# A small two-layer network inside a long kernel: its first layer in single-pass matmuls, with the operands split into high and low parts beforehand

## The reference, cut to what matters

```
def compress_tokens(t, pos_emb, w1, w2):
    ...
    blocks = jnp.concatenate([chunks[:, :, i:i + n_cmp] for i in range(r)], axis=3)
    blocks = (blocks + pos_emb).reshape(B, G, n_cmp, CMP_BLOCK * dh)
    return jax.nn.gelu(blocks @ w1) @ w2
```

## Time and profile before

| | us |
|---|---|
| median of the runs | 964.74 |
| the profiled execution, its own time | 964.92 |
| its span | 962.7 |
| PE busy in the span | 946.2 (98%) |
| DVE, ACT, POOL busy | 569.4, 419.7, 369.0 |

### The profile page before, as it was taken

How to read it: one execution, slowest core, us unless ns; L and a number is a source line. 1 busy time by engine, 2 the same in 40 slices (tenths; PEclk the granted TensorE clock), 3 DMA queues, 4 the chain that set the end, 5 groups by cost and what they waited for, 6 DMA issues and landing times.

```text
span 962.7 us, 14693 instructions
## 1 busy us (share of the span) xinstructions
PE 946.2 (98%) x5579; PEld 823.8 (86%) x5579; DVE 569.4 (59%) x1083; ACT 419.7 (44%) x730; POOL 369.0 (38%) x442
## 2 busy tenths in 40 slices
PE   9999999999999999999999999999999999999997
PEld 8878887878888898688888888888999999988886
DVE  2764445388554356384558743888899999711114
ACT  5334325265555263345464633544444444433332
POOL 5771551246435454122223036597000000366561
PEclk9999999999999999999999999999999999999999
DMA  7374243112144252231211112226322442122312
GB/s 234 120 199 99 66 143 99 45 44 66 44 147 160 70 175 66 76 122 45 72 62 65 45 44 89 74 69 213 116 89 89 128 136 88 46 88 91 124 47 88
DMA packets 74758, 93.44 MB, mean 97 GB/s; under 512 B 15332, under 2 KB 53777, under 8 KB 74688
## 3 DMA queue, kind: packets, MB, share of 16 engines
q1 hardware_dynamic: 74256, 91.91, 29.9%
q10 hardware_dynamic: 432, 0.59, 0.2%
HBM read 90.09 MB, written 7.12 MB: 101 GB/s over the span
## 4 chain that ended last, share of the span: by engine, by line
PE 90%; DVE 4%; ACT 2%; issue 2%; DMA 1%; POOL 0%; SPq 0%; DVEq 0%; POOLq 0%; ACTq 0%
PE psum L1360 52%; PE psum L1421 17%; PE psum L1701 6%; PE psum L1661 4%; PE psum L1676 3%; PE psum L1753 1%; PE psum L1487 1%; PE psum L1627 1%; PE psum L1729 1%; PE psum L1743 1%; PE psum L1714 1%; DMA RAW<-in_w_in_dram 1%; PE psum L1640 1%; PE psum L1799 0%; DVE R L2730 0%
## 5 line engine op out<-in xcount | busy, mean ns | idle before, releaser
L1360 PE MATMUL psum<-WR,XT 128*128 128x512 f32 (+3 forms) x1620 | 390.5, 387 | 1.0 <-ACT R L1031 0.7
L2756 POOL TENSOR_TENSOR WR<-RAW,WR 128x256 fp32r<-128x256 f32 (+3 forms) x320 | 259.9, 841 | 321.0 <-ACT WR L1859 320.9
L1360 PEld LDWEIGHTS psum<-WR,XT 128*128 128x128 f32 x1620 | 285.9, 188 | 51.5 <-issue 4.1
L2756 POOL TENSOR_TENSOR WR<-RAW_B,WR 128x256 fp32r<-128x256 f32 x88 | 71.6, 837 | 202.7 <-ACT WR L1859 202.7
L1859 ACT ACTIVATE WR<-RAW 128x512 fp32r<-128x512 f32 (+3 forms) x160 | 93.4, 603 | 83.5 <-PE psum L1360 69.4
L1360 PE MATMUL psum<-WR,TT 128*128 128x512 f32 x528 | 119.9, 389 | 0.0
L1360 PEld LDWEIGHTS psum<-WR,TT 128*128 128x128 f32 x528 | 99.0, 188 | 20.5
L2034 ACT ACTIVATE prob<-prob,st 128x512 f32<-128x512 f32 (+2 forms) x112 | 58.4, 545 | 92.6 <-DVE st L2418 83.5
L1701 PEld LDWEIGHTS psum<-ones_up,probT 128*128 128x128 f32 x536 | 70.7, 191 | 7.1 <-issue 1.3
L1701 PE MATMUL psum<-ones_up,probT 128*128 128x128 f32 x536 | 72.7, 275 | 0.1
L1421 PE MATMUL psum<-TT,WR 128*128 128x256 f32 x576 | 71.7, 283 | 0.0
(11 more groups left out here) (292 smaller groups left out, 1254.0 us busy)
## 6 DMA issues: line engine op xcount, KB each, us to landing
RAW<-in_w_gate_up_dram SPq DMA_DIRECT2D x28, 512.0 KB, 5.0
RAW<-in_w_in_dram SPq DMA_DIRECT2D x13, 1024.0 KB, 5.2
RAW_B<-in_w_down_dram SPq DMA_DIRECT2D x11, 1024.0 KB, 5.0
RAW<-in_w_out_dram SPq DMA_DIRECT2D x8, 1024.0 KB, 5.3
RAW_B<-in_w_gate_up_dram SPq DMA_DIRECT2D x16, 512.0 KB, 6.0
RAW<-in_w_in_dram SPq DMA_DIRECT2D x13, 512.0 KB, 4.9
rep_scratch<-rows_scratch SPq DMA_DIRECT2D x12, 320.0 KB, 6.6
RAW<-in_w_in_dram SPq DMA_DIRECT2D x4, 768.0 KB, 4.3
```

The lines of the kernel that those rows point to most:

```text
L1360: last = pe.matmul(outp, stationary(x), moving(y), start=start and n == 0, stop=stop and n == 2)
L2756: last = pool.tensor_tensor(WR[:, s % RING, 1, lo:hi], raw[:, raw_half[g], q, lo:hi], WR[:, s % RING, 0, lo:hi].bitcast(F32), ALU.subtract)
```

## The change

- `hidden` is made of fp32r matmuls: the stationary operand is now 128 x 128, with the 64 columns of the blocks' high part beside the 64 of their low part, and the moving operand is once the high and once the low part of the `w1` piece. 16 pieces by 2 matmuls for each of k and v. The result has 128 rows: the lower 64 come from the blocks' high part and the upper 64 from their low part, and they have to be added.
- New steps `bp v`: ScalarE copies the high part of the blocks of k or v (128 x 1024), VectorE subtracts for the low part.
- New steps `w1 pair`, 16 of them: ScalarE copies two pieces' high part (128 x 512), VectorE subtracts for the low part, in place over `w1`. Pairs 0 to 7 are k, 8 to 15 v. `PLAN` puts 0 to 7 at quarters 16, 19, ... 37 of `in2` and 8 to 15 at 62 to 69.
- After part 1 of `hidden`: ScalarE copies rows 64 to 127 out, VectorE adds rows 0 to 63, ScalarE then takes the gelu (before: the gelu straight from PSUM).
- `qt cmp` and `blocks` stand two quarters earlier, `hidden` at (64, 66, 69, 72) where it was (64, 65, 67, 69), `hid_t` at (69, 75) where it was (67, 72). `w1` of k and v change places in SBUF, and so in the order of their DMAs.

```diff
     if kind == "hidden":
         kv, part = at
-        return [("hidden", kv, 0)] if part else [("hidden", 0, 1)] if kv else [("blocks",)]
+        out = [("w1", 4 * (2 * kv + part) + 3)]
+        return out + ([("hidden", kv, 0)] if part else [("hidden", 0, 1)] if kv else [("blocks",), ("bp", 1)])
+    if kind == "w1":
+        pair = at[0]
+        return ([("w1", pair - 1)] if pair else []) + ([("hidden", 0, 0)] if pair >= 12 else [("bp", pair // 2 - 4)] if pair >= 8 else [])
...
-                index["out1", 1, 0]: [load_x_again, lambda: load_w1(1)],
-                index["in2", 1, 0]: [lambda: load_w1(0)],
+                index["out1", 1, 0]: [load_x_again, lambda: load_w1(0)],
+                index["in2", 1, 0]: [lambda: load_w1(1)],
...
                     if part == 0:
                         wait_sc(step)
-                        pe.wait_ge(s_w1[kv], 16)
-                        pe.wait_ge(blk_done, 1)
+                        pe.wait_ge(blk_done, kv + 1)
+                    pe.wait_ge(w1_lo_done, 4 * (2 * kv + part) + 4)
                     for m in range(8 * part, 8 * part + 8):
-                        last = pe.matmul(SC[nth["hidden", kv, 0] % 2][0:64, 0:256], blocks[:, kv, m, :], w1[kv][:, m, :],
-                                         start=m == 0, stop=m == 15)
-                    if part:
-                        last.then_inc(sc_in, 1)
+                        for x, moving in enumerate((hi_of_w1(16 * kv + m), w1_lo[kv][:, m, :])):
+                            last = pe.matmul(SC[nth["hidden", kv, 0] % 2][:, 0:256], block_parts[kv][:, m, :, :].rearrange("p x n -> p (x n)"), moving,
+                                             start=(m, x) == (0, 0), stop=(m, x) == (15, 1))
+                    last.then_inc(sc_in if part else w1_used, 1)
...
+                elif what == "w1":
+                    pair = step[1]
+                    kv, m = divmod(2 * pair, 16)
+                    act.wait_ge(s_w1[kv], 16)
...
+                    if pair in (8, 10):
+                        act.wait_ge(blk_done, pair // 2 - 3)
+                    if pair == 12:
+                        act.wait_ge(w1_used, 1)
+                    act.activation(hi_of_pair(pair), w1[kv][:, m:m + 2, :], ACT.Copy).then_inc(w1_hi_done, 1)
+                elif what == "bp":
+                    v = step[1]
+                    act.wait_ge(blk_raw, v + 1)
...
+                    act.activation(block_parts[v][:, :, 0, :], blocks[:, v, :, :], ACT.Copy).then_inc(blk_hi, 1)
                 elif what == "hidden" and step[2]:
                     kv = step[1]
                     act.wait_ge(sc_in, nth["hidden", kv, 0] + 1)
-                    if kv == 0:
-                        act.wait_ge(tr_in, nth["qt", "cmp", 3] + 1)
-                    act.activation(hid_nat[0:64, kv, :], SC[nth["hidden", kv, 0] % 2][0:64, 0:256], ACT.Gelu_apprx_tanh).then_inc(hid_act, 1)
+                    act.activation(hid_nat[0:64, kv, :], SC[nth["hidden", kv, 0] % 2][64:128, 0:256], ACT.Copy).then_inc(hid_low, 1)
+
+                    act.wait_ge(sc_out, nth["hidden", kv, 0] + 1)
+                    act.activation(hid_nat[0:64, kv, :], hid_nat[0:64, kv, :], ACT.Gelu_apprx_tanh).then_inc(hid_act, 1)
```

More of the change, by code:

```diff
@@ L301, in make_timeline @@
         "OS": 1.5, "CS_b": 1.5, "F": 2, "sp_b": 2.5, "S": 3, "Z": 3, "sp": 4, "qt": 4.5,
-        "gx": 4.2, "xt": 4.4, "blocks": 5, "hidden": 6, "hid_t": 6.5, "gelu": 6, "cmpkv": 7, "gm_w": 8, "gm_a": 9, "gm": 10,
+        "gx": 4.2, "xt": 4.4, "blocks": 5, "bp": 5.2, "w1": 5.5, "hidden": 6, "hid_t": 6.5, "gelu": 6, "cmpkv": 7, "gm_w": 8, "gm_a": 9, "gm": 10,
     }
@@ L461, in make_timeline @@
         on(PLAN["hidden"][n], ("hidden", n // 2, n % 2))
+    for n in range(2):
+        on(PLAN["bp"][n], ("bp", n))
+    for pair in range(16):
+        on(PLAN["w1"][pair], ("w1", pair))
     for n in range(2):
@@ L997, in ones_and_v, with hi_of_w1, hi_of_pair @@
             return ones_up[:, 0:2 * at_].rearrange("p (x n) -> p x n", x=2)[:, :, 0:HD]
+        def hi_of_w1(n):
+            part, slot = ((1, 0), (0, 0), (0, 4), (2, 0), (3, 0), (3, 4), (0, 0), (0, 4))[n // 4]
+            return w1_hi[part][:, slot + n % 4, :]
+        def hi_of_pair(pair):
+            part, slot = ((1, 0), (0, 0), (0, 4), (2, 0), (3, 0), (3, 4), (0, 0), (0, 4))[pair // 2]
+            return w1_hi[part][:, slot + 2 * pair % 4:slot + 2 * pair % 4 + 2, :]
         def bias_of(name, h, i, m):
@@ L1258, in load_w1 @@
             def load_w1(kv):
-                if kv:
+                if not kv:
                     sp.wait_ge(tr_in, nth["F", 3, 2] + 1)
@@ L2055, in _ @@
                     take_transposed(act, step)
+                elif what == "w1":
+                    pair = step[1]
+                    kv, m = divmod(2 * pair, 16)
+                    act.wait_ge(s_w1[kv], 16)
+                    if pair == 0:
+                        act.wait_ge(sq_done, nth["sq", "in2", 3] + 1)
+                        act.wait_ge(gx_done, nth["gx", "in2", 3, 1] + 1)
+                    if pair in (8, 10):
[6 more added lines that the diff above has]
+                    act.wait_ge(blk_raw, v + 1)
+                    if v == 0:
+                        act.wait_ge(tr_in, nth["qt", "cmp", 3] + 1)
+                    act.activation(block_parts[v][:, :, 0, :], blocks[:, v, :, :], ACT.Copy).then_inc(blk_hi, 1)
                 elif what == "hidden" and step[2]:
@@ L2510, in _ @@
                                 last = dve.tensor_tensor(dst, s_, pp, ALU.add)
-                    last.then_inc(blk_done, 1)
+                        last.then_inc(blk_raw, 1)
+                elif what == "bp":
+                    v = step[1]
+                    dve.wait_ge(blk_hi, v + 1)
+                    dve.tensor_tensor(block_parts[v][:, :, 1, :], blocks[:, v, :, :], block_parts[v][:, :, 0, :].bitcast(F32),
+                                      ALU.subtract).then_inc(blk_done, 1)
+                elif what == "w1":
+                    pair = step[1]
+                    kv, m = divmod(2 * pair, 16)
+                    dve.wait_ge(w1_hi_done, pair + 1)
+                    dve.tensor_tensor(w1_lo[kv][:, m:m + 2, :], w1[kv][:, m:m + 2, :], hi_of_pair(pair).bitcast(F32),
+                                      ALU.subtract).then_inc(w1_lo_done, 1)
                 elif what == "hidden" and step[2]:
-                    dve.wait_ge(hid_act, step[1] + 1)
-                    dve.sem_inc(sc_out, 1)
+                    kv = step[1]
+                    dve.wait_ge(hid_low, kv + 1)
+                    dve.tensor_tensor(hid_nat[0:64, kv, :], SC[nth["hidden", kv, 0] % 2][0:64, 0:256], hid_nat[0:64, kv, :],
+                                      ALU.add).then_inc(sc_out, 1)
                 elif what == "hid_t":
```

22 lines of the change are left out of this document (17 added, 5 removed).

## The result

The changed kernel takes 974.94 us (median of four runs, 974.08 to 975.25), the kernel before 964.86 (four runs, 964.64 to 964.97): a ratio of 1.0103 [1.0086, 1.0121], 10.1 us slower. The direction was as forecast, the size was not: 4.1 us were forecast, and 974.9 lies outside 965.5 to 972.0.

What follows compares the result with a forecast made beforehand. TensorE was taken to bound the kernel, busy 946.2 of 962.7 us. Waits of 10.8 us less 6.7 us gained in `hidden` make +4.1, so 968.8 us, range 965.5 to 972.0.

Steps and rivals of the forecast that it cites:

- 1 chunk 0 to 1: At chunk 0's evacuation, split copies and subtractions queued ahead delay the first tiles on ScalarE and VectorE: 1.4 us.
- 2 `qt q 0`: At the first `qS` transpose, TensorE waits for chunk 1's tile 0, queued behind ScalarE's late `w1` copies: 0.6 us.
- 3 `qt q 1`: At the second `qS` transpose, TensorE waits for VectorE's subtractions, two tiles and `qS` copy: 0.7 us.
- 4 `qt q 3`: At the fourth `qS` transpose, TensorE waits for row copy, table load, sum, gelu and `qS` copies: 3.0 us, the largest.
- 5 `hid_t 0`: Behind the fourth `qS` transpose, its `qS` copies outlast the `hidden` matmuls running beside them: 0.8 us.
- 6 `qt slc 1`: At the second `kS_slc` transpose, no quarter covers copy, sum, gelu and the first transpose's copies: 2.0 us.
- 7 `hid_t 1`: Right behind `qt slc 2`, TensorE waits 1.0 us for copies, where it waited 0.5 before: cost 0.5 us.
- 8 `CS 0`: Ahead of `CS 0`, nothing covers VectorE placing the second layer's results: 2.3 us less 0.5 before, 1.8 us.
- first rival: VectorE and GpSimd block each other at chunk 0's evacuation; tile 1 starts 1.9 us later, 970.7 us; 0.19 shared with slower matmuls.
- rival with 384-column time: `hidden` matmuls paced like 384-column ones, gain 3.2 us instead of 6.7, up to 972.3 us; 0.19 shared with GpSimd lock.
- Hand-overs hidden: TensorE's work between transposes covers most of the ScalarE and VectorE waits, 7.6 us coming to nothing: 961.2 us; chance 0.13.
- Given back later: TensorE idle time elsewhere that hangs on its own clock, such as DMAs, absorbs the shift: no change, 964.8 us; chance 0.06.

Runs made afterwards that it cites:

- `fill`: Changed kernel plus 28 matmuls whose result nobody reads, ahead of the three long TensorE waits; 970.31 us, ratio 1.0058 to the kernel before.
- `plan2`: Changed kernel with another placing of the same steps and SP's bias loads behind chunk 3's first weight load; 967.55 us, ten runs.
- `order`: Kernel before, fp32 matmuls and no splits, with only the new places of `qt cmp`, `blocks`, `hidden` and `hid_t`; 972.56 us, ratio 1.0076.
- `plan3`: Changed kernel with steps placed so no idle times stand close together, `CS` from 83, bias loads behind the weight load; 963.80 us, ratio 0.9991.
- `keep`: Changed kernel, splits and single-pass matmuls kept, with `hidden` and `hid_t` back at their old places; 971.21 us, ratio 1.0068.
- `nov`: Changed kernel without the value weights' eight split pairs; `hidden` of the values uses the keys' parts, so values are wrong; 970.24 us, ratio 1.0064.
- `plan1`: Changed kernel with the same steps placed to give each transpose a quarter or more of cover, `CS` from 84; 974.62 us, ratio 1.0095.
- `plan1b`: `plan1` with SP's eight bias loads moved behind chunk 3's first weight load; 968.25 us, ratio 1.0042.
- `plan2f`: `plan2` plus 15 matmuls whose result nobody reads, ahead of four waiting TensorE instructions; 964.88 us, ratio 1.0000.

## Why the prediction came out as it did

| step | forecast | changed kernel | `fill` (clock at 1.00) |
|---|---|---|---|
| 1 chunk 0 to 1 | 1.4 | 1.4 | 1.4 |
| 2 `qt q 0` | 0.6 | 0.74 | 0.72 |
| 3 `qt q 1` | 0.7 | 0.68 | 0.68 |
| 4 `qt q 3` | 3.0 | 3.22 | 3.39 |
| 5 `hid_t 0` | 0.8 | 0 | 0.88 |
| 6 `qt slc 1` | 2.0 | 2.09 | 2.34 |
| 7 `hid_t 1` | 0.5 | 0.53 | 0.53 |
| 8 `CS 0` | 1.8 | 1.86 | 2.05 |
| sum of the waits | 10.8 | 10.5 | 12.0 |
| gain of `hidden` | -6.7 | -5.4 | -6.7 |
| what is left, half clock above all | 0 | 5.2 | 0 |
| shift of the far block | 4.1 | 10.3 | 5.3 |

For the changed kernel the gain is 1.3 less, since one part took 3.24 us, and 5.2 is what is left of the 10.3. For `fill` the wait of steps 4, 6 and 8 is the filling and the wait left behind it together (2.92 + 0.47, 2.10 + 0.24, and 2.09 + 0.47 less the 0.51 of before); the same wait unfilled reads about 0.2 less, because the profile counts idle time from the modelled end of a matmul. Its sum is 12.0 - 6.7 = 5.3, and `CS 0` was 5.32 late. The walk itself can so be followed to the tenth at full clock, and there it was 1.2 us short, over steps 2, 4, 5, 6 and 8.

*The step that failed* is the one that sums: waits of 10.8, "less 6.7 it makes +4.1 us". It priced an idle stretch of TensorE at its length and all matmuls behind it at the pace of the earlier trace rows. Nothing in the forecast, neither a term, nor a rival, nor the range, spoke of TensorE's clock, though the rows of before give it in a column of its own (1.00). The three stretches of step 4, 6 and 8 each brought the fall with them. That is 4.6 us of the 6.1 by which the forecast was short, as `fill` shows by the times; `plan2` with its two groups of runs bears the cause out. Most of the other 1.5 is the 1.2 by which the walked waits were short.

*Step 1* came out as forecast, at 1.4 us. TensorE in the changed kernel:

```profile
359.52 0.93 PE L1390 MATMUL psum<-WR,XT 128*128 128x512 f32 x3 [0.94 <-ACT st L1061]
361.04 4.49 PE L1390 MATMUL psum<-WR,XT 128*128 128x512 f32 x18 [0.59 <-DVE st L1061]
```

It waits 0.94 us for tile 0 and 0.59 for tile 1. Tile 0's quarter starts at 359.52, 0.63 after its 358.89; tile 1's at 361.04, in the kernel before at 359.65, three matmuls behind 358.89: 1.39 us late. The walk had 1.0 and then 0.4 more, so the sum is right in part by luck. VectorE in the changed kernel:

```profile
356.43 3.09 DVE L2574 TENSOR_TENSOR w_k_lo<-w_k,w_hi_a 128x512 fp32r<-128x512 f32 x3 [0.35 <-ACT w_hi_a L2098]
359.44 0.47 DVE L1061 TENSOR_SCALAR cmp_nat<-psum,st 128x256 f32<-128x256 f32 x1
```

The first three subtractions took 0.69 each, but the last three 3.09 us together (0.80, 1.23 and 1.22), so VectorE came to tile 1 at 359.44 where the walk had 359.2. That is the first rival's mechanism at a small part of its price of 1.9 us: the rival had all six at 1.28. GpSimd is slower beside them too: its nine splits from 353.57 on take 8.61 us, where before ten from 353.74 on took 6.78. The Trainium skill, SBUF — State Buffer, "SBUF: two separate sides", would have each wait out a GpSimd instruction; GpSimd was at work without a break from 353.6 on, and two of the subtractions behind that (354.34 and 355.38) still took 0.69, so the trace agrees in part only.

*Step 4* is right in its pieces too. ScalarE in the changed kernel:

```profile
392.08 0.38 ACT L2109 ACTIVATE hid_nat<-psum 64x256 f32<-64x256 f32 x1
392.48 1.28 ACT L2112 ACT_TABLE_LOAD   x1
394.15 0.42 ACT L2112 ACTIVATE hid_nat<-hid_nat 64x256 f32<-64x256 f32 x1 [0.39 <-DVE hid_nat L2579]
394.59 1.19 ACT L1955 ACTIVATE qS<-psum 64x512 fp32r<-64x512 f32 x2
```

Copy, table load, gelu behind VectorE's sum, then `qS`: these were walked to end at 391.9, 393.2, 393.9 and 395.0 and end 0.6 to 0.8 later, as TensorE itself comes to its wait 0.6 later (394.1 for 393.5). The 1.4 us more that the forecast worked out beside step 4 for the table load did not come: the copy ends and the load begins 0.02 us behind it.

*The matmuls* of 256 columns take 0.120 us at full clock, as the 1344 do, so the rival with 384-column time is out. *Hand-overs hidden* is out: in `fill` none of the waits fell away, and `order` shows four of them without any split. *Given back later* did not occur for the loss (the shift only grows behind `CS 0`), but 5.2 of some 6.1 us of gain were lost behind it in `plan3`.

*What the forecast left unseparated:* it walked splits and places as one. `order` shows that 5.1 us of the waits and 2.3 of half clock come with the places alone, 1.73 of them at step 4, which the forecast had put down to the splits, the sum and the table load. The old places of the transposes had quarters between them, and `hidden` parts of 3.6 us as cover; the new ones have `slc 0` and `slc 1` back to back and nothing in front of `CS 0`.

Open: why the clock falls behind 1.39 us in one kernel and not behind 2.09 in another; and what sets the waits behind `CS 0` once the work in front is shorter.

## What to carry to other kernels

Where a change makes TensorE wait for some microseconds, even in several short waits, in a stretch that it kept busy before, price the work behind the wait at both clock levels: here 7.7 us of long waits cost 4.6 us more, and a few matmuls that nobody reads took that back. Work of TensorE that is made shorter had been cover for other engines' chains; count who runs beside it before booking the gain, and look at the cover behind it too. When a step is moved, read who else waits for its end: here SP's queue held the next weights back behind it, and ScalarE waited 9.2 us for them. For all the work on places, the best variant gained 1.0 us.

## What the runs showed of the hardware

- TensorE fell to 1.2 GHz in or behind single idle stretches of 1.39 to 5.25 us, or three of about 1 us close together, in a program that kept it 97% busy, and stayed there for 3 to 10 us. Behind other single stretches of 1.73 (`order`), 1.90 (`keep`) and 2.09 us (`nov`) it did not fall. The longest stay in the changed kernel (10.2 us) stands behind its third wait, of 2.37 us; the two before it brought 3.4 us each.
- The fall is not the same in each run of one program: `plan2` ran in two groups some 3 us apart. `nov`, `keep`, `plan1` and `plan1b` spread over 3 to 5 us, the changed kernel and `order`, with long waits too, over 1.2 and 1.4, `plan2f` over 0.4.
- At half clock a 128x256 matmul is recorded at 415 ns instead of 283 and its weight load at 330 instead of 192; sixteen take 3.24 us in line (with the clock coming back within them) instead of 1.92.
- A VectorE subtraction of 512 columns with both inputs in SBUF took 0.68 to 0.80 us or 0.98 to 1.23 in the changed kernel; the slow ones all had GpSimd's subtractions of the ring beside them, but so had some of the fast ones. GpSimd's own took 0.96 us on average there (nine in 8.61), before 0.68 (ten in 6.78).
